# Two-layer hybrid encoder with eight experts: row counts in registers, another order of PE's expert code, and finer signals

## The chip, the cores and the metric

The kernel runs on one core of one Trainium2 chip. The metric is the device time of one execution in microseconds (us), as the median of several runs. TensorE is called PE here, VectorE DVE, ScalarE ACT, GpSimd POOL, and SP is the engine that issues most DMAs.

## What is computed

Two layers over 256 tokens of width 1024 in float32. Each layer has a token mixer (differential attention, an mLSTM and latent attention side by side) and a channel mixer. The second layer's channel mixer is the part that the change touches: each token goes to the best two of eight experts, and an expert is a SwiGLU of inner width 3584.

```python
def swiglu(u, wg, wu, wd):
    return (jax.nn.silu(u @ wg) * (u @ wu)) @ wd

    logits = (t @ w_router).astype(jnp.float32) + b_router.astype(jnp.float32)
    top_val, top_idx = lax.top_k(logits, TOP_K)
    gates = jax.nn.softmax(top_val, axis=-1)
...
        return swiglu(xblk, w_gate_e[e], w_up_e[e], w_down_e[e])
...
    y = jnp.zeros((n, d), h.dtype).at[tok_sorted].add(yb[dest] * g_sorted[:, None].astype(h.dtype))
```

Only the rows that chose an expert have to pass through it, but all of its weights do: 42 transfers of 1 MB an expert, 336 in all.

## The kernel before

The program is written engine by engine, and each engine runs its own instructions in the order in which they are written. Engines meet at semaphores alone: `then_inc` raises one when an instruction is done, `wait_ge` holds the engine until a value is reached.

**Routing.** Ahead of the experts, PE gathers the 512 chosen rows (two of each token) with selection matrices into eight PSUM banks (L1387). ACT copies the even banks into `xs`, DVE the odd ones (L1930 and L2542), and both raise `xs_ready`. The counts of rows of the experts stand in `cnt`, the first rows in `first`. POOL waits for eight `xs_ready`, and for each expert copies its rows, up to 256, from `xs` into `xe` (L2772) and raises `xe_ready`. In the profile `xs` shows as arena, `xe` as mixT.

**Which code an expert runs.** PE, ACT and DVE each hold six bodies of code, for up to 32, 64, 128, 160, 192 and 256 rows (`NVAR`), made by `experts` (L669). For each expert an engine jumps to "next", adds one to a register, jumps to "pick", loads the expert's count from `cnt` into a register (L684), and goes through a chain of tests ("tree") to the body that fits. The body of `first_variant`, 128 rows on all three engines, stands right behind the tests; the others follow in order of size. Each body begins with a hint for its own last jump, the one back to "next".

**A body.** It walks 14 stages of 256 inner columns. A stage's weights are three transfers into a ring of 14 slots of 1 MB: ("gu", s, 0) and ("gu", s, 1) hold gate and up for the upper and lower half of the 1024 inputs, ("down", s) the down product. Up to 64 rows PE works in plain float32 (`expert_whole`: gate and up at L1443, a turn at L1429, down at L1455). With more rows the weights are split into a high and a low part by ACT and DVE, and PE makes three products with 128-row or with wide tiles (`expert_split`, L1565 and L1613; `expert_wide`, L1484 to L1528). In both the first stage's gate and up is made whole (L1578, L1484).

**SP** issues the 42 transfers of an expert in a loop over the experts. Ahead of each it waits until the slot's last use is over (`last_use`, L789): a "down" block by `down_done`, both "gu" blocks of a stage by `gu_full`, which PE raises when the whole gate and up product of that stage is done.

## Time and profile before

| | us |
|---|---|
| median of 3 runs | 1678.16 (1676.92 to 1680.18) |
| profiled execution | 1674.14 |
| its span, first to last instruction | 1672.3 |
| PE busy with matmuls | 1478.1 (88%) |
| ACT busy | 589.6 (35%) |
| DVE busy | 781.4 (47%) |
| DMA of expert weights | 336 transfers of 1 MB |

Times of the trace are from the start of the span. The experts begin at about 680 us and end at about 1645. With these inputs the eight experts have, in order, up to 32, 32, 128, 64, 160, 32, 192 and 64 rows, which is seen in the shapes of PE's rows: 128x32 by 128x128 for 32 rows, 128x64 by 128x256 for 64, 128x512 for 128, and 128x160 and 128x192 for the wide ones. A row of the timeline merges equal instructions that follow each other. In brackets stands the idle time of the engine just before, and what ended it; "issue" is time in which the engine waited for nothing that the profile shows.

### The profile page before, as it was taken

The numbers are of one execution on the slowest core, as the hardware profiler recorded it, in microseconds if no ns is written. First come the engines' busy times: TensorE is split into PE (matmuls) and PEld (weight loads), VectorE is DVE, ScalarE is ACT, GpSimd is POOL, SyncE is SP. The second block draws the span as 40 slices with busy tenths as digits, with TensorE's granted clock in tenths as the row PEclk, the third lists the DMA queues.
The fourth block names the chain that finished last, engine by engine and source line by source line (L and its number), as shares of the span: only waits on it lengthen the run. The fifth ranks groups of instructions, "written<-read, shape, count | busy, mean of one in ns | idle before, by whom it ended". The sixth has DMA issues, their size and how long they took to land.

```text
span 1672.3 us, 30627 instructions
## 1 busy us (share of the span) xinstructions
PE 1478.1 (88%) x12402; PEld 1185.7 (71%) x12403; DVE 781.4 (47%) x1097; ACT 589.6 (35%) x793; POOL 69.4 (4%) x66
## 2 busy tenths in 40 slices
PE   5999899999999998756579999999996679999894
PEld 3878778999977886644458875588985468888452
DVE  2584565565546655100028851177761036665112
ACT  2445253444344432100027740156551025554101
POOL 0010100000010111000000000000000000000002
PEclk8999999999999999987789999999998789999998
DMA  9644467745433528899999999997567996555893
GB/s 362 236 161 175 192 229 291 287 170 196 158 100 123 227 76 362 350 424 424 424 424 426 426 410 426 424 406 285 236 281 306 424 424 245 225 226 227 328 426 151
DMA packets 69183, 488.89 MB, mean 292 GB/s; under 512 B 7744, under 2 KB 7776, under 8 KB 11168
## 3 DMA queue, kind: packets, MB, share of 16 engines
q1 hardware_dynamic: 66800, 479.94, 71.0%
q10 hardware_dynamic: 1648, 4.59, 0.8%
q8 instruction: 117, 1.92, 0.5%
q0 software_dynamic: 576, 2.10, 0.4%
q14 instruction: 42, 0.34, 0.1%
HBM read 482.66 MB, written 3.93 MB: 291 GB/s over the span
## 4 chain that ended last, share of the span: by engine, by line
PE 44%; DMA 9%; issue 4%; DVE 2%; SPq 1%; ACT 1%; POOL 1%; ACTq 0%; POOLq 0%; DVEq 0%
PE PG L1443 9%; DMA ring<-in_experts 6%; PE PG L1500 4%; PE Y L1528 4%; PE Y L1455 4%; PE TRB L1500 4%; PE PG L1565 4%; DMA arena<-in_experts 3%; PE TRB L1506 3%; PE PG L1506 3%; PE Y L1613 2%; PE Y L1519 2%; PE TRB L1429 2%; SPq L786 1%; PE Y L1252 1%
## 5 line engine op out<-in xcount | busy, mean ns | idle before, releaser
L2570 DVE COPY arena<-TRB 128x64 f32<-128x64 f32 (+1 forms) x70 | 17.6, 251 | 343.0 <-PE TRB L1429 343.0
L1443 PE MATMUL PG<-ring,mixT 128*32 128x128 f32 (+1 forms) x1920 | 117.4, 352 | 65.2 <-issue 60.6
L1677 ACT ACTIVATE rope<-PG 64x128 f32<-64x128 f32 (+2 forms) x84 | 27.2, 324 | 378.7 <-PE PG L1443 356.2
L1443 PEld LDWEIGHTS PG<-ring,mixT 128*32 128x32 f32 (+1 forms) x1920 | 90.6, 139 | 95.9 <-issue 81.4
L1677 ACT ACTIVATE parts<-ring 128x2048 fp32r<-128x2048 f32 x81 | 151.8, 1901 | 9.1 <-DMA ring<-in_weights 4.0
L945 PE MATMUL PG<-h_parts,parts 128*128 128x512 f32 x432 | 152.9, 394 | 1.4 <-DVE arena L2448 1.4
L1443 PE MATMUL PG<-arena,mixT 128*32 128x128 f32 (+1 forms) x1664 | 102.2, 353 | 42.0 <-issue 42.0
L1443 PEld LDWEIGHTS PG<-arena,mixT 128*32 128x32 f32 (+1 forms) x1664 | 79.2, 140 | 69.4 <-issue 56.3
L947 PE MATMUL PG<-h_parts,parts 128*128 128x256 f32 x432 | 121.9, 282 | 0.0
L2433 DVE TENSOR_TENSOR parts<-ring,parts 128x2048 fp32r<-128x2048 f32 x42 | 95.1, 2289 | 30.4 <-ACT parts L1677 30.4
L2554 DVE TENSOR_TENSOR parts<-arena,parts 128x2048 fp32r<-128x2048 f32 x42 | 95.2, 2287 | 17.0 <-PE Y L1519 14.4
L2554 DVE TENSOR_TENSOR ring_parts<-ring,parts 128x2048 fp32r<-128x2048 f32 x39 | 88.4, 2287 | 24.2 <-PE Y L1519 13.3
L945 PEld LDWEIGHTS PG<-h_parts,parts 128*128 128x128 f32 x432 | 81.2, 188 | 19.8 <-DVE arena L2448 1.6
L947 PEld LDWEIGHTS PG<-h_parts,parts 128*128 128x128 f32 x432 | 81.3, 188 | 0.0
L1677 ACT ACTIVATE parts<-arena 128x2048 fp32r<-128x2048 f32 x42 | 78.9, 1902 | 4.2 <-PE PG L1565 4.1
L912 PE MATMUL Y<-parts 128*128 128x256 f32 x224 | 63.5, 284 | 0.2 <-DVE parts L2457 0.2
L913 PE MATMUL Y<-parts 128*128 128x256 f32 x224 | 63.4, 283 | 0.0
L914 PE MATMUL Y<-parts 128*128 128x256 f32 x224 | 63.4, 283 | 0.0
L2123 DVE TENSOR_TENSOR ring_parts<-ring,ring_parts 128x2048 fp32r<-128x2048 f32 (+1 forms) x24 | 52.8, 2199 | 18.9 <-ACT ring_parts L1677 18.8
L2554 DVE TENSOR_TENSOR parts<-arena,scr_parts 128x2048 fp32r<-128x2048 f32 x21 | 48.1, 2292 | 26.6 <-ACT scr_parts L1677 26.6
L1455 PE MATMUL Y<-arena 128*32 128x256 f32 (+1 forms) x512 | 57.2, 450 | 1.8 <-DMA arena<-in_experts 1.8
L1677 ACT ACTIVATE ring_parts<-ring 128x2048 fp32r<-128x2048 f32 (+1 forms) x24 | 43.8, 1837 | 41.4 <-PE Y L1252 30.2
(384 smaller groups left out, 2839.8 us busy)
## 6 DMA issues: line engine op xcount, KB each, us to landing
ring<-in_experts SPq DMA_DIRECT2D x168, 1024.0 KB, 17.1
arena<-in_experts SPq DMA_DIRECT2D x168, 1024.0 KB, 18.9
ring<-in_weights SPq DMA_DIRECT2D x116, 1024.0 KB, 6.4
ring<-in_weights SPq DMA_DIRECT2D x4, 512.0 KB, 5.1
ypairs<-hT ACTq DMA_DIRECT2D x3, 512.0 KB, 7.0
tok<-in_x SPq DMA_DIRECT2D x1, 1024.0 KB, 9.0
result<-scr SPq DMA_DIRECT2D x2, 512.0 KB, 2.6
ring<-in_weights SPq DMA_DIRECT2D x2, 432.0 KB, 6.2
```

Source lines behind the costliest of these rows:

```text
L912: mm(out_, w_hi[w][:, c], x[0], start=first, stop=False, skip_group_check=True)
L945: mm(PG[:, m, :].rearrange("p (i t) -> p i t", i=2), w_hi[d % SPLITS][:, c], h_parts[:, :, k, :], start=(k == 0), stop=False, skip_group_c ...
L947: last = mm(PG[:, m, 0:T], w_lo[d % SPLITS][:, c], h_hi[:, k, :], start=False, stop=(k == KD - 1), skip_group_check=True)
L1443: last = mm(bank[i * n:(i + 1) * n, 0:width], xe[:, k, 0:n], w[k // 4][:, k % 4, i * width:(i + 1) * width], start=(k == 0), stop=(k == KD ...
L1455: last = mm(o, actT[:, s % 2, f, 0:n], w[:, f, c:c + width], start=(s == 0 and f == 0), stop=(s == STAGES - 1 and f == 1))
L1500: last = mm(both, hi[:, k, i // 2, i % 2, :], h_parts[:, :, h * KD // 2 + k, 0:n], start=(h == 0 and k == 0), stop=False, skip_group_check ...
L1506: last = mm(bank[:, 0:n], lo[:, k, i // 2, i % 2, :], h_parts[:, 0, h * KD // 2 + k, 0:n], start=False, stop=(h == 1 and k == KD // 2 - 1) ...
L1528: last = mm(o, a[:, s % 2, f, :], w[:, f, c:c + width], start=(opens and s == 0 and f == 0), stop=(closes and s == STAGES - 1 and f == 1))
L1565: last = mm(bank, x[j][:, h * KD // 2 + k, :], w[:, k, :], start=(opens and k == 0), stop=(closes and k == KD // 2 - 1))
L1677: return nc.scalar.activation(out_, in_, func, **kw)
L2433: V.tensor_tensor(w_lo[d % SPLITS], ring[:, slot_of[slot_of_dense(d)], :, :].rearrange("p k c -> p (k c)"), w_hi[d % SPLITS].bitcast(F32), ...
L2554: V.tensor_tensor(w_lo_e[q % SLOTS_E], ring_e[q % SLOTS_E].rearrange("p k c -> p (k c)"), w_hi_e[q % HI].bitcast(F32), ALU.subtract).then_ ...
```

## The change

1. **Counts in registers.** `experts` loads all eight counts into eight registers at the start. "next" adds one and moves each count one register down, and jumps straight to the tests. "pick" is gone. This holds for PE, ACT and DVE.
2. **32 rows behind PE's chain.** On PE, `first_variant` is 32: the tests ask for 256, 192, 160, 128 and 64 rows in turn, and the 32-row body follows them. ACT and DVE keep 128.
3. **A second hint.** On PE each body ends with a hint for the last test of the chain (`closest`), just ahead of the jump back. In the built program this test jumps to the 64-row body and falls through to the 32-row one.
4. **First rows in two pieces.** `xs_ready` becomes `xs_even` and `xs_odd`. Ahead of its loop POOL copies the first expert's rows as six of eight slices, then two, each when its banks are copied. The loop makes seven copies in place of eight.
5. **First blocks by own signal.** PE raises the new `gu_half` once the upper half of a stage's gate and up is done. SP waits for it ahead of refilling a ("gu", s, 0) slot, and DVE's `low_rows_of(0)` waits for it in place of `hi_used`. In the split and wide bodies the first stage's `hi_used` is raised one bank or one matmul earlier.

```diff
-            rows = eng.alloc_register(label("rows"))
+            to_come = [eng.alloc_register(label(f"rows_{i}")) for i in range(NE)]
+            rows = to_come[0]
+            for i in range(NE):
+                eng.reg_load(to_come[i], cnt[0:1, i:i + 1])
             eng.reg_mov(turn, 0)
-            eng.br(label("pick"))
+            eng.br(label("tree"))
             with nc.body(label("next"), valid_engines=own):
                 eng.reg_add(turn, turn, 1)
-                eng.br_lt(turn, NE, on_true=label("pick"), on_false=label("done"))
-            with nc.body(label("pick"), valid_engines=own):
-                e = eng.snap(turn, min_val=0, max_val=NE - 1)
-                eng.reg_load(rows, cnt[0:1, bass.ds(e, 1)])
-                eng.br(label("tree"))
+                for i in range(NE - 1):
+                    eng.reg_mov(to_come[i], to_come[i + 1])
+                eng.br_lt(turn, NE, on_true=label("tree"), on_false=label("done"))
...
-                        eng.br_lt(rows, NVAR[NVAR.index(n) - 1] + 1, on_true=then, on_false=label(n))
+                        closest = eng.br_lt(rows, NVAR[NVAR.index(n) - 1] + 1, on_true=then, on_false=label(n))
...
                     emit(eng.snap(turn, min_val=0, max_val=NE - 1), n)
+                    if name == "pe":
+                        closest.branch_hint(eng.mark_branch_hint_location())
                     eng.br(label("next")).branch_hint(back)
...
-                kind, s = expert_list[(i - SLOTS_E) % USES][0:2]
+                kind, s, *half = expert_list[(i - SLOTS_E) % USES]
+                if half == [0]:
+                    return gu_half, e * STAGES + ((STAGES if i >= SLOTS_E else 0) + s + 1)
...
+            pe.sem_inc(gu_half, STAGES)
...
+                        if k == KD // 2 - 1:
+                            last.then_inc(gu_half, 1)
...
-            experts(pe, "pe", expert)
+            experts(pe, "pe", expert, first_variant=32)
...
-                        ve.wait_ge(hi_used, e * USES + 1)
+                        ve.wait_ge(gu_half, e * STAGES + (STAGES + 1))
...
-            po.wait_ge(xs_ready, KD)
+            po.wait_ge(xg_full, KD)
+            rows = xs[:, 0:KD * PAIRS].rearrange("p (k s) -> p k s", k=KD)
+            for a, b in ((0, KD - 2), (KD - 2, KD)):
+                po.wait_ge(xs_even, b // 2)
+                po.wait_ge(xs_odd, b // 2)
+                last = G.tensor_copy(xe[:, a:b, :], rows[:, a:b, 0:T])
+            last.then_inc(xe_ready, 1)
             po.wait_ge(table_ready, 1)
-            with po.Fori(0, NE) as e:
-                start = po.value_load(first[0:1, bass.ds(e, 1)], min_val=0, max_val=PAIRS)
-                po.wait_ge(gu_full, e * FT + FT)
+            with po.Fori(0, NE - 1) as e:
+                start = po.value_load(first[0:1, bass.ds(e + 1, 1)], min_val=0, max_val=PAIRS)
+                po.wait_ge(gu_full, e * FT + 2 * FT)
```

How this stands on PE, from the last gather to the body behind the tests. Each row is the source line, the operation, its operands and how many follow each other. Before, with the 128-row body (L1578) behind the tests:

```order
1935 L1387 MATMUL TRB<-parts,h_parts 128x512 x8
1936 L678 UNCONDITIONAL_BRANCH
1937 L680 REGISTER_ALU
1938 L681 COMPARE_AND_BRANCH
1939 L683 ISA
1940 L684 TENSOR_LOAD cnt
1941 L685 UNCONDITIONAL_BRANCH
1942 L692 COMPARE_AND_BRANCH x2
1943 L694 COMPARE_AND_BRANCH x3
1944 L697 BRANCH_PREFETCH_HINT
1945 L698 ISA
1946 L1415 ISA
1947 L1578 MATMUL PG<-ring,mixT 128x512 x8
```

The same place now, with the 32-row body (L1451 now, L1443 before):

```order
1934 L1395 MATMUL TRB<-parts,h_parts 128x512 x8
1935 L680 TENSOR_LOAD cnt x8
1936 L682 UNCONDITIONAL_BRANCH
1937 L684 ISA
1938 L687 COMPARE_AND_BRANCH
1939 L696 COMPARE_AND_BRANCH x5
1940 L699 BRANCH_PREFETCH_HINT
1941 L700 ISA
1942 L1423 ISA
1943 L1451 MATMUL PG<-ring,mixT 32x128 x64
```

The load of a count has left the way from one expert to the next, and the 32-row body has taken the place of the 128-row body. The end of a body on PE shows the new hint; now the 32-row body's last product, its jump back, and the 64-row body that follows it:

```order
2015 L1465 MATMUL Y<-arena 32x256 x8
2016 L702 BRANCH_PREFETCH_HINT
2017 L703 UNCONDITIONAL_BRANCH
2018 L699 BRANCH_PREFETCH_HINT
2019 L700 ISA
2020 L1423 ISA
2021 L1451 MATMUL PG<-ring,mixT 64x256 x32
```

On POOL, ahead of the experts, the first copy is now in two pieces outside the loop (L2784), ahead of the load of `first`:

```order
35 L2777 MEMSET arena 128x512
36 L2784 COPY mixT<-arena 128x1536
37 L2784 COPY mixT<-arena 128x512
38 L2787 UNCONDITIONAL_BRANCH
39 L2787 ISA
40 L2788 TENSOR_LOAD first
```

Before, the loop began there, and its load and its copy of 128x2048 were the first.

The built program holds 64 bytes an instruction. The bodies of PE have 2,359 instructions for 32 rows, 1,293 for 64, 1,135 for 128, 2,677 for 160 and 2,454 for 192 before, each one or two more now.

## Rows read from the trace of the kernel before

**Rows 1.** From the page: its first line, and the queue that brings instructions
```profile
span 1672.3 us, 30627 instructions
...
q8 instruction: 117, 1.92, 0.5%
```

**Rows 2.** Timeline of PE, the first matmuls of each expert: start, us, what, [idle before]
```profile
679.85 5.25 PE L1443 MATMUL PG<-ring,mixT 128*32 128x128 f32 x128 [4.54 <-POOL mixT L2772]
...
766.11 6.84 PE L1443 MATMUL PG<-ring,mixT 128*32 128x128 f32 x128 [7.53 <-issue]
...
866.64 8.82 PE L1578 MATMUL PG<-ring,mixT 128*128 128x512 f32 x16 [2.44 <-issue]
...
991.03 7.13 PE L1443 MATMUL PG<-ring,mixT 128*64 128x256 f32 x64
...
1078.80 2.44 PE L1484 MATMUL PG<-mixT,ring 128*128 128x160 f32 x16
...
1265.14 6.13 PE L1443 MATMUL PG<-ring,mixT 128*32 128x128 f32 x128 [10.23 <-issue]
...
1352.08 4.53 PE L1484 MATMUL PG<-mixT,ring 128*128 128x192 f32 x16 [7.20 <-issue]
...
1559.60 9.14 PE L1443 MATMUL PG<-ring,mixT 128*64 128x256 f32 x64 [5.61 <-issue]
```

**Rows 3.** Stretches: length, busy PE, PEld, DVE, ACT, POOL, PE clock, DMA share, GB/s
```profile
680.00:690.00 10.00, 9.53 (x244) 8.50 (x244) 1.33 (x5) 2.09 (x4) 0.00 (x0) 0.85 0.52 201
690.00:700.00 10.00, 9.03 (x222) 6.55 (x214) 1.56 (x6) 0.81 (x3) 0.00 (x0) 1.00 1.01 424
...
980.00:990.00 10.00, 8.96 (x40) 7.13 (x39) 5.63 (x6) 2.69 (x3) 2.42 (x1) 1.00 1.01 413
990.00:1000.00 10.00, 10.00 (x85) 6.50 (x85) 1.84 (x4) 2.63 (x4) 0.00 (x0) 1.00 0.97 371
...
1265.00:1270.00 5.00, 4.86 (x92) 4.89 (x96) 0.00 (x0) 1.12 (x1) 0.00 (x0) 0.50 0.10 15
...
1345.00:1350.00 5.00, 0.00 (x0) 0.00 (x0) 1.80 (x3) 1.99 (x3) 0.00 (x0) 0.53 1.01 421
```

**Rows 4.** Chain of waits in the fourth expert: start, us, what
```profile
1040.66 3.45 PE PG L1443 x32
...
1046.62 3.47 PE PG L1443 x32
...
1052.60 1.25 issue
1053.86 3.67 PE PG L1443 x32
...
1060.04 1.14 issue
...
1067.35 1.11 issue
```

**Rows 5.** Timeline, all engines, the start of the fifth expert
```profile
1085.42 2.34 PE L1484 MATMUL TRB<-mixT,ring 128*128 128x160 f32 x16
...
1090.39 1.44 PE L1500 MATMUL PG<-h_parts,parts 128*128 128x320 f32 x8 [2.63 <-DVE rope L2601]
```

**Rows 6.** Timeline, the sixth expert: SP's first transfers and PE's last product
```profile
1268.97 7.65 SPq L786 DMA_DIRECT2D ring<-in_experts  x7
...
1343.81 1.07 PE L1455 MATMUL Y<-arena 128*32 128x256 f32 x16 [1.64 <-DMA arena<-in_experts]
```

**Rows 7.** Timeline, the sixth expert: weight loads (PEld) of one product
```profile
1277.75 1.31 PEld L1443 LDWEIGHTS PG<-arena,mixT 128*32 128x32 f32 x41
...
1280.54 0.59 PEld L1443 LDWEIGHTS PG<-arena,mixT 128*32 128x32 f32 x23 [1.49 <-issue]
```

**Rows 8.** Timeline ahead of the first expert: last gathers, copies, SP's first transfers
```profile
673.29 2.02 PE L1387 MATMUL TRB<-parts,h_parts 128*128 128x512 f32 x8
...
675.35 0.69 DVE L2542 COPY arena<-TRB 128x512 f32<-128x512 f32 x1 [1.17 <-PE TRB L1387]
677.71 1.89 POOL L2772 COPY mixT<-arena 128x2048 f32 x1 [23.60 <-issue]
...
683.56 7.42 SPq L786 DMA_DIRECT2D ring<-in_experts  x7
```

More of the change, by code:

```diff
@@ L589, in build @@
         xg_full = sem("xg_full")
-        xs_ready = sem("xs_ready")
+        xs_even, xs_odd = sem("xs_even"), sem("xs_odd")
+        gu_half = sem("gu_half")
         pad_zero = sem("pad_zero")
@@ L1486, in gate_up_whole @@
                             if i == 2:
-                                used = last
-                        (used if h else last).then_inc(hi_used, 1)
-                    last.then_inc(gu_full, 2)
+                                last.then_inc(hi_used, 1)
+                        last.then_inc(gu_full if h else gu_half, 2 if h else 1)
                 def gate_up_half(s, h):
@@ L1507, in gate_up_half @@
                                       start=False, stop=(h == 1 and k == KD // 2 - 1), skip_group_check=True)
-                    if h == 1:
-                        last.then_inc(gu_full, 2)
+                    last.then_inc(gu_full if h else gu_half, 2 if h else 1)
                 def down_rest(s):
@@ L1581, in gate_up_first @@
                                 last.then_inc(gu_full, step)
-                        (before if h else last).then_inc(hi_used, 1)
+                        before.then_inc(hi_used, 1)
+                        if h == 0:
+                            last.then_inc(gu_half, 1)
                 def gate_up(s):
@@ L1603, in gate_up_half @@
                     lo_ready(e, q)
-                    gate_up_part(s, h, x_hi, w_lo_e[q % SLOTS_E], closes=(h == 1))
+                    last = gate_up_part(s, h, x_hi, w_lo_e[q % SLOTS_E], closes=(h == 1))
+                    if h == 0:
+                        last.then_inc(gu_half, 1)
                 def down_part(s, a, w, opens=False, closes=False):
@@ L1927, in _ @@
                 ae.wait_ge(xg_full, k + 1)
-                run(xs[:, k * PAIRS:(k + 1) * PAIRS], xg_banks[k], ACT.Copy).then_inc(xs_ready, 1)
+                run(xs[:, k * PAIRS:(k + 1) * PAIRS], xg_banks[k], ACT.Copy).then_inc(xs_even, 1)
             for b in range(TB):
@@ L1931, in _ @@
             ae.wait_ge(table_ready, 1)
-            ae.wait_ge(xs_ready, KD)
+            ae.wait_ge(xs_even, KD // 2)
+            ae.wait_ge(xs_odd, KD // 2)
             def silu(e, n, u, m):
@@ L2541, in _ @@
                 ve.wait_ge(xg_full, k + 1)
-                V.tensor_copy(xs[:, k * PAIRS:(k + 1) * PAIRS], xg_banks[k]).then_inc(xs_ready, 1)
+                V.tensor_copy(xs[:, k * PAIRS:(k + 1) * PAIRS], xg_banks[k]).then_inc(xs_odd, 1)
             def gated(e, n, u, m):
@@ L2648, in expert_split @@
                 ve.sem_inc(conv_lo, 2)
-                ve.wait_ge(hi_used, e * USES + 1)
+                ve.wait_ge(gu_half, e * STAGES + (STAGES + 1))
                 low_rows_of(0)
```

## Prediction

> **What bounds the kernel now.** I read four views, in this order. The page first: one execution spans 1672.3 us [rows 1]. The rows of TensorE (PE) at the eight places where an expert begins [rows 2] then give the row counts of the experts by their shapes (32, 32, 128, 64, 160, 32, 192 and 64) and the idle time ahead of each: 4.54, 7.53, 2.44, none, none, 10.23, 7.20 and 5.61 us. Nothing in the profile is waited for in most of that ("issue"). The table of stretches says which of these gaps cost anything [rows 3]: weights come at 424 GB/s and the DMA engines are full (1.01) from 690 us on, still so at 980 and again at 1345; they idle in part at 680 to 690 (201 GB/s), a little at 990 to 1000 (0.97), and nearly wholly at 1265 to 1270 (0.10). So:
> - experts 1 and 2 are bound by DMA: their end is set by when the transfers restart near 683 us. The 7.53 us gap between them is hidden.
> - expert 3 (128 rows) is bound by PE from its first matmul. Expert 4 (64 rows) is too, until DMA is late three times: its stages begin 5.96 us apart (1040.66, 1046.62), then 7.24, with 1.25, 1.14 and 1.11 us of idle [rows 4]. PE alone would end it 3.5 us earlier.
> - expert 5 (160) is PE's own, and its start hangs on ScalarE and VectorE: PE has its four banks done about 1087.7 us but waits for VectorE until 1090.39 [rows 5], some 2 us of slack.
> - expert 6 (32 rows) is bound by DMA, which stood still before it: its first weights are asked for at 1268.97, and PE waits for the last at 1343.81 [rows 6]. Experts 7 and 8 are PE's. So the gaps of 10.23, 7.20 and 5.61 us all cost time, the 2.44 one too.
>
> **What a gap is made of.** The code of an expert has to be brought in: the instruction queue made 117 transfers of 1.92 MB, 16.4 KB each [rows 1]. The built program has 64 bytes an instruction, so a transfer brings a block of 256. PE stops after 41 of 64 loads in the middle of one product and goes on 1.49 us later with nothing to wait for [rows 7]. That is a block boundary reached before its block. Counted in the built program it is the 335th load of the 32-row code, and all boundaries follow from it. The 128-row code stands right behind the tests and its gap is 2.44 us; from the same 32-row code to a 32-row code that stands elsewhere it is 7.53. **A jump to code that is not there costs 7.53 - 2.44 = 5.1 us** (P). 10.23 us is more than that. The 160-row code jumps back 14 instructions behind a boundary, the other bodies 81 to 165, so there the hint given at the body's start can do little. **A late jump back costs 10.23 - 7.53 = 2.7 us** (B), and up to P while the DMA engines are full.
>
> [...]
>
> **The change part by part.**
> 1. First rows in two pieces. The copy of all rows took 1.89 us from 677.71, after the last VectorE copy ended at 676.04 [rows 8]. Now six of eight slices go once PE's last gather is done (673.29 + 2.02 = 675.3), about 1.45 us, then two in about 0.55 us (estimates from 1.89 us for eight, plus 0.1): ready near 677.4 against 679.6. The register load and the address work that stood ahead are gone too. PE starts 2.2 us sooner. Eight register loads at the start lie on PE behind queued gathers, and on ScalarE and VectorE before 681, when the first product is whole.
> 2. First blocks by own signal. SP may refill a slot after half a product instead of a whole one. Two products took 5.25 us [rows 8], so this is 1.3 to 1.6 us more; the first transfer goes from 683.56 [rows 8] to about 679.8. **Experts 1 and 2 end 3.8 us earlier** (ends: 2.2 and 4.6; 201 of 424 GB/s in ten us leaves 5.3 to gain). In steady DMA it gives nothing.
> 3. 32 rows behind the tests. The bodies of the built program now end 32 (32 rows), 47, 160, 24 and 176 instructions behind a boundary, against 137, 151, 81, 14 and 165. For 32 rows this boundary is 2 or 3 instructions behind the last wait for weights, so the jump back is late each time; before it was early.
>  - 32 to 32: hidden, as before.
>  - **32 to 128** was 2.44. It loses the place behind the tests (+5.1) and its early jump back (+2.7 to +5.1), less 0.4 for the register load (an estimate; no row shows one, and it is 0 to 2.44): +7.4 to +9.8, I take +8.2, nearer B since the block asked for meanwhile saves a little. Queued on PE behind it is expert 3, all of PE's, so nothing hides it.
>  - 128 to 64, 64 to 160: no jump fetches now. The 64-row code begins in the block where the 32-row code ends, and the 160-row code where the 128-row code ends. A late jump back after 64 rows, a little over 1 us beyond what is queued, falls into the 2 us of slack. ScalarE's way to expert 5 is 0.4 us shorter. Expert 4's late weights: half a product of 3.62 us and fuller slots take 2.4 of its 3.5 us.
>  - **160 to 32** was 10.23. The code follows the tests, but only 24 instructions of it lie in that block, and the next must come too; the second hint may put another transfer ahead of it. Between nothing and P is saved, plus 1.5 for the half signal (half of 3.1 us, from 6.84 us for two products [rows 2]): 1.5 to 6.6, I take 4.0.
>  - **32 to 192** was 7.20 and holds P already; add a late jump back: +2.3 to +4.7, with DMA full [rows 3] I take +3.6.
> 4. Second hint. The built program puts the last test's jump on 64 rows, so the hint names the 64-row code. **192 to 64** was 5.61: its block is asked for at the jump back, instead of another block first: -0.4 to -5.6, I take -2.4, since the transfer still has to come. A block of instructions has no row of its own, so this is a choice near the middle.
>
> Sum: -3.8 + 8.2 - 2.4 - 0.4 (to expert 5's end: +1.6) - 4.0 + 3.6 - 2.4 = **-1.2 us**. The profiled execution took 1674.14 us, 1.8 around its span, so 1672.9; it lies 4.0 under the median of 1678.16, and the difference, not the level, is forecast: 1677.0 us.
>
> **Rivals.**
> - A, slower. The jumps out of 32-row code are late at the full price. B is P when the DMA engines are full, and the block behind the tests costs as much as the jump did: +9.8, +4.7, -1.5 in place of +8.2, +3.6, -4.0: +5.2 more, 1682. For it: both jumps fall where the DMA share is 1.01 [rows 3]. Against: 7.53 was paid at the same share. It decides from B of about 4 us.
> - B, faster. The nearer hint brings the tests' block in time and the late jumps back vanish, or the boundaries lie a few instructions elsewhere: 2.7 less after each of two 32-row bodies, and 2 more after 160 rows: 1669.6. For it: four of the seven jumps back were in time. Against: the count.
> - C, slower. At 64 to 160 the 160-row code's block is no longer kept: it is ten transfers old, where it was the next block before. That is +5.1 and 1 us, less 1.7 of slack: 1681.4. For it: the 192-row code, twelve blocks back, paid 7.20. [...]
> - D. The change moves code and nothing of it shows at the end, since what the 32-row bodies gain the others lose: this is my sum itself.
>
> **How the numbers follow.** Forecast, with D in it, 0.45 (its own range 1674 to 1680), A 0.17, B 0.30, C 0.08. Leaving out a tenth at each side gives 1668.5 to 1684. A measurement tells 0.2%, 3.4 us, from no change. Faster: B and a little of the forecast, 0.32. Slower: A, C and a little, 0.24. Same: 0.44.
>
> **What would show it.** First PE matmul of expert 1 near 677.7 and SP's first transfer near 679.8. Idle ahead of the 128-row code of 10 us or more, of the 192-row code over 10, of the 64-row code at the end near 3, of the last 32-row code from 10.2 to about 7. Expert 3 begins about 4 us later than 866.64, expert 5 about 2 later than 1078.8. If the gap at 128 rows stays under 7 us, the count of boundaries is wrong and B holds; if a gap of 5 us opens at or shortly behind the 160-row code's start, C does; if the 32-row code stops after its first 20 matmuls for 5 us, A does.

## Result: 0.81% slower, and the profile after

Each kernel was timed several times beside the kernel before. The changed kernel takes 1695.15 us (median of 9 runs) against 1680.19 (9 runs); the ratio is 1.0081 with a 95% interval of 1.0062 to 1.0100, so 13.6 us **slower**. The forecast was 1.2 us faster, in a range that ended 5.8 us above the median of before; the result lies outside it.

The spans of the two profiled executions differ by more, 1672.3 against 1693.3 us, since the profiled execution of before was 6.0 us under its median and that of after on it. Part of the difference arises ahead of all that the change touches: PE's gathers began at 667.58 us before and at 669.75 after, and in the profiles of the experiments anywhere from 667.75 to 675.96. So starts are counted from the first gather on, and places are compared by their gaps.

The page of after: as many matmuls, and four blocks of instructions fewer.

```profile
span 1693.3 us, 30716 instructions
...
PE 1477.2 (87%) x12402; PEld 1183.5 (70%) x12402; DVE 781.6 (46%) x1096; ACT 589.9 (35%) x793; POOL 69.4 (4%) x67
...
q8 instruction: 113, 1.85, 0.4%
```

How much a transfer of that queue brings is seen in the trace of before, between the start of its second transfer and of its 37th, where PE has no record of a jump (columns as in [rows 3], then the queue):

```profile
43.52:657.98 614.46, 591.14 (x4417) 502.97 (x4416) 360.21 (x576) 253.79 (x401) 42.41 (x35) 0.99 0.51 194
...
q8 instruction: 35, 0.57, 0.4%
```

The matmuls and weight loads alone are 252 a transfer, and all records of PE with its waits and register instructions, 9,023, are 258. In the 160-row body, from 1087.47 to 1233.08 us, nine transfers began over 2,258 records, 251 each. So I take 256 instructions for a block of 16,384 bytes, 64 bytes each, and the stops lie where this puts them (e3). The bodies have their counted lengths in the trace too: from the hint at a body's start to the add behind its jump back there are 2,361 records of PE for 32 rows, 1,286 for 64, 1,118 for 128, 2,682 for 160 and 2,455 for 192, within 1.5% of the built program's counts (a trace can lack some records).

The timeline of PE in after, the first matmuls of each expert, which answers to [rows 2] (start, us, what, [idle before]):

```profile
679.92 1.03 PE L1451 MATMUL PG<-ring,mixT 128*32 128x128 f32 x10 [2.39 <-POOL mixT L2784]
683.65 4.87 PE L1451 MATMUL PG<-ring,mixT 128*32 128x128 f32 x118 [2.69 <-issue]
...
766.20 1.03 PE L1451 MATMUL PG<-ring,mixT 128*32 128x128 f32 x10 [6.47 <-issue]
772.36 4.89 PE L1451 MATMUL PG<-ring,mixT 128*32 128x128 f32 x118 [5.13 <-issue]
...
878.35 10.19 PE L1586 MATMUL PG<-ring,mixT 128*128 128x512 f32 x16 [12.38 <-issue]
...
1004.08 7.13 PE L1451 MATMUL PG<-ring,mixT 128*64 128x256 f32 x64
...
1099.32 4.22 PE L1494 MATMUL PG<-mixT,ring 128*128 128x160 f32 x16 [10.07 <-issue]
...
1280.05 0.63 PE L1451 MATMUL PG<-ring,mixT 128*32 128x128 f32 x10 [4.33 <-issue]
1286.83 5.35 PE L1451 MATMUL PG<-ring,mixT 128*32 128x128 f32 x118 [6.15 <-issue]
...
1374.70 5.19 PE L1494 MATMUL PG<-mixT,ring 128*128 128x192 f32 x16 [11.96 <-issue]
...
1580.66 8.81 PE L1451 MATMUL PG<-ring,mixT 128*64 128x256 f32 x64 [3.39 <-issue]
```

Three things are new in it. Ahead of the third expert stand 12.38 us in place of 2.44, ahead of the seventh 11.96 in place of 7.20. Ahead of the fifth, where there was no gap, stand 10.07. And each 32-row body stops after ten matmuls. Ten matmuls are 20 instructions (each has a weight load), with four others ahead of them behind the tests, which is where the block that holds the tests ends by the forecast's count. Place by place, in us of the two profiled executions:

| | before | after | difference | forecast |
|---|---|---|---|---|
| start of the gathers | 667.58 | 669.75 | +2.2 | 0 |
| gathers to the end of expert 2 | 196.6 | 196.2 | -0.4 | -3.8 |
| gap ahead of expert 3 | 2.44 | 12.38 | +9.9 | +8.2 |
| expert 3 | 124.4 | 125.7 | +1.3 | 0 |
| expert 4 | 87.8 | 85.2 | -2.6 | -2.4 |
| gap ahead of expert 5 | 0 | 10.07 | +10.1 | 0 |
| expert 5 | 176.1 | 176.4 | +0.3 | -0.4 |
| gap ahead of expert 6, and expert 6 | 90.0 | 87.0 | -3.0 | -4.0 |
| gap ahead of expert 7 | 7.20 | 11.96 | +4.8 | +3.6 |
| expert 7 | 201.9 | 202.6 | +0.7 | 0 |
| gap ahead of expert 8 | 5.61 | 3.39 | -2.2 | -2.4 |
| expert 8 and the end | 112.7 | 112.6 | -0.1 | 0 |

The differences add up to 21.0, while the medians are 15.0 apart: the table tells where time went, not how much of it to the microsecond. One line was not forecast at all, the 10.1 us ahead of the fifth expert.

### The profile page after: what moved, and what is told of

The parts are those of the page before. It is cut to its first block, busy times and chain, and to the rows that moved or that the text cites. A ratio compares the mean times of both kernels' runs of the same rounds, so it can differ in the third digit from the quotient of the medians.

```text
span 1693.3 us, 30716 instructions
## 1 busy us (share of the span) xinstructions
PE 1477.2 (87%) x12402; PEld 1183.5 (70%) x12402; DVE 781.6 (46%) x1096; ACT 589.9 (35%) x793; POOL 69.4 (4%) x67
## 4 chain that ended last, share of the span: by engine, by line
PE 45%; DMA 9%; issue 5%; DVE 2%; POOL 1%; ACT 1%; SPq 0%; POOLq 0%; ACTq 0%; DVEq 0%
PE PG L1451 9%; DMA arena<-in_experts 6%; PE PG L1509 4%; PE Y L1465 4%; PE Y L1536 4%; PE TRB L1509 4%; PE PG L1573 4%; DMA ring<-in_experts 3%; PE TRB L1515 3%; PE PG L1515 3%; PE Y L1625 2%; PE Y L1527 2%; PE TRB L1437 2%; PE PG L1494 1%; PE Y L1260 1%
## 5 line engine op out<-in xcount | busy, mean ns | idle before, releaser
L1451 PE MATMUL PG<-ring,mixT 128*32 128x128 f32 (+1 forms) x1920 | 115.5, 339 | 61.8 <-issue 59.4
L1451 PEld LDWEIGHTS PG<-ring,mixT 128*32 128x32 f32 (+1 forms) x1920 | 86.9, 133 | 94.0 <-issue 76.4
L1451 PE MATMUL PG<-arena,mixT 128*32 128x128 f32 (+1 forms) x1664 | 99.5, 344 | 43.8 <-issue 43.8
L1451 PEld LDWEIGHTS PG<-arena,mixT 128*32 128x32 f32 (+1 forms) x1664 | 76.8, 136 | 70.9 <-issue 57.8
L2136 DVE TENSOR_TENSOR ring_parts<-ring,ring_parts 128x2048 fp32r<-128x2048 f32 (+1 forms) x24 | 52.8, 2199 | 18.9 <-ACT ring_parts L1689 18.8
L1689 ACT ACTIVATE arena<-PG 128x512 f32<-128x512 f32 x29 | 17.4, 598 | 114.5 <-PE PG L955 105.6
```

Source lines behind the costliest of these rows:

```text
L1451: last = mm(bank[i * n:(i + 1) * n, 0:width], xe[:, k, 0:n], w[k // 4][:, k % 4, i * width:(i + 1) * width], start=(k == 0), stop=(k == KD ...
L1689: return nc.scalar.activation(out_, in_, func, **kw)
```

## Experiments

All twelve ran beside the kernel before; us are the ratio less one times 1680. The intervals are 2 to 4 us to each side, so two of these kernels are told apart by their times alone only where they differ by some 4 to 5 us.

| | ratio (95% interval) | us |
|---|---|---|
| changed kernel | 1.0081 (1.0062 to 1.0100) | +13.6 |
| e1_first128 | 0.9998 (0.9980 to 1.0016) | -0.3 |
| e2_onehint | 1.0080 (1.0057 to 1.0103) | +13.4 |
| e3_padded | 1.0003 (0.9986 to 1.0020) | +0.5 |
| e4_before_late | 1.0057 (1.0040 to 1.0074) | +9.6 |
| e5_signals | 0.9969 (0.9951 to 0.9987) | -5.2 |
| e6_registers | 0.9983 (0.9965 to 1.0000) | -2.9 |
| e7_no_order_no_hint | 0.9969 (0.9953 to 0.9985) | -5.2 |
| e8_tests_in_bodies | 0.9873 (0.9849 to 0.9896) | -21.3 |
| e9_160_behind_64 | 1.0040 (1.0023 to 1.0058) | +6.7 |
| e10_tests_unpadded | 0.9925 (0.9911 to 0.9939) | -12.6 |
| e11_all_engines | 0.9843 (0.9824 to 0.9862) | -26.4 |
| e12_e7_padded | 0.9946 (0.9925 to 0.9966) | -9.1 |

### Which part costs

**e1_first128**, the order alone undone.

```diff
-            experts(pe, "pe", expert, first_variant=32)
+            experts(pe, "pe", expert)
```

> The changed kernel with the 128-row body behind PE's tests again; all other parts of the change stay. Theory M (code blocks: a block of PE's code that is not there costs about 5 to 6 us while weights stream, and the new order of the bodies makes more of them be missed): the gap ahead of the third expert falls from 12.38 to about 2.5 us, that ahead of the fifth from 10.07 to none, that ahead of the seventh from 11.96 to about 7.2, and 10.2 us stand ahead of the sixth again. The time lies 3 to 7 us under the kernel before. Rival U (the cost comes from the other parts: registers, pieces, signals): the time stays 10 us or more over the kernel before.

Measured: 13.9 us less than the changed kernel, level with the kernel before. The order (part 2) carries the whole loss; theory M stands, U falls. The gaps came back as expected, none ahead of the fifth expert, 9.91 us ahead of the sixth and 7.67 ahead of the seventh. But the 3 to 7 us of gain did not come. The timeline of PE shows where one part of it went, in the 128-row body behind the tests (the stretch shown ends after 100 of the first row's 128 matmuls):

```profile
685.63 4.58 PE L1451 MATMUL PG<-ring,mixT 128*32 128x128 f32 x100 [5.39 <-issue]
...
871.46 4.55 PE L1586 MATMUL PG<-ring,mixT 128*128 128x512 f32 x10 [0.95 <-DMA ring<-in_experts]
881.44 5.28 PE L1586 MATMUL PG<-ring,mixT 128*128 128x512 f32 x6 [5.42 <-issue]
```

After ten matmuls a block ends, and PE stops for 5.42 us. The kernel before ran through the same place [rows 2]. The first line shows the other part: PE's first product waits for its jump, not for POOL.

**e7_no_order_no_hint**, the second hint taken out of e1.

```diff
-                    if name == "pe":
-                        closest.branch_hint(eng.mark_branch_hint_location())
```

> Parts 1, 4 and 5 (registers, pieces, signals), with the 128-row body behind PE's tests and one hint, as before. Theory H1 (a hint that is armed takes the place of the next block in order): the stop of 5.42 us in the 128-row code of e1_first128, after its tenth matmul, is gone, and so are 3 to 5 us of its time; the gap ahead of the last expert stays at 5.2 to 5.6. 3 to 5 us under the kernel before. Rival: the stop is of the moved block boundary alone; it stays, and the time is that of e1_first128.

Measured: 0.9969, 4.9 us less than e1 (just clear of the noise of the two), and the sixteen matmuls stand in one row:

```profile
867.37 7.13 PE L1584 MATMUL PG<-ring,mixT 128*128 128x512 f32 x16 [1.22 <-DMA ring<-in_experts]
```

The rival falls. The transfers of PE's code show the order: in e1 three blocks were brought here, beginning at 867.73, 873.45 and 879.05 us, in e7 two, at 863.68 and 869.24. The third of e1 began 3.0 us after PE had stopped (876.01). So I read it as follows: an armed hint takes the place of the next block in order. It is given at a body's end, the tests' block is entered, the hint's target is asked for, and the block right behind the tests is asked for only when PE stands at its border. That the block at 873.45 is the hint's target is inferred, since a transfer doesn't tell which block it brings.

**e2_onehint**, the same edit on the changed kernel.

> The changed kernel without the second hint. Theory H1 (the hint for the 64-row code takes the place of the next block in order): the 32-row code still stops after 10 matmuls, but for 2.5 to 3.5 us in place of 5.13 and 6.15, the gap ahead of the last expert rises from 3.39 to about 5.6, and the sum is 0 to 3 us less than the changed kernel. Rival H2 (the second hint is what makes the jumps back late): the jumps back after 32 rows cost about 1 us, the gap ahead of the third expert falls from 12.38 to about 8, and the time is over 10 us less than the changed kernel. Rival H3: the hint does nothing, all gaps stay within 0.5 us.

Measured: 1.0080, as the changed kernel. The single places came out near what H1 said (the rows from the second on):

```profile
678.40 3.70 PE L1449 MATMUL PG<-ring,mixT 128*32 128x128 f32 x128 [2.39 <-POOL mixT L2782]
...
765.96 5.23 PE L1449 MATMUL PG<-ring,mixT 128*32 128x128 f32 x118 [3.01 <-issue]
...
873.12 9.95 PE L1584 MATMUL PG<-ring,mixT 128*128 128x512 f32 x16 [12.92 <-issue]
...
1276.81 5.79 PE L1449 MATMUL PG<-ring,mixT 128*32 128x128 f32 x118 [2.28 <-issue]
...
1574.46 9.13 PE L1449 MATMUL PG<-ring,mixT 128*64 128x256 f32 x64 [6.19 <-issue]
```

The stops after ten matmuls fall from 5.13 to 3.01 and from 6.15 to 2.28, the last gap rises from 3.39 to 6.19. In this order the hint gives 2.8 us at one jump and takes 3.9 inside the sixth body. H2 falls with the 12.92: the jumps back are late without it too. The first row shows what H1 had not named: the first body's stop of 2.69 us is gone as well. SP's first transfer came 11.4 us behind the gathers in place of 15.6, and the second expert ended 191.9 us behind them in place of 196.2. At that place no body had given a second hint yet, so the reading above does not explain it; what ties this stop to the hint is open. The 4 us that this trace gains there are not seen in the ratio, and lie within the noise of the two (5 us).

**e5_signals**, parts 4 and 5 on the kernel before (`experts` as before, all else as changed).

> The kernel before with parts 4 and 5 alone (first rows in two pieces, first blocks by own signal). By the forecast: PE starts 2.2 us sooner, SP 3.8 us sooner, the third expert begins 3.8 us sooner, and 3 to 6 us are gained in all. Rival S1: the first 32-row product waits for the jump instead, which took 6.05 us and ends at 678.2 in the kernel before, 1.4 us ahead of the copy: then PE starts 1 to 1.5 us sooner and 1 to 3 us are gained. Rival S2: within 1 us of the kernel before, since the weights are late at the fourth expert whatever happens at the first.

Measured: 0.9969, 5.2 us faster (2.2 to 8.2), around the forecast's 3 to 6. Counted from the gathers at 672.24, SP's first transfer came 13.1 us behind them (16.0 before, 15.6 in the changed kernel) and PE's first matmul 11.0 (12.3 before). But the third expert began only 2.1 us sooner, not 3.8, so the total fits better than its parts. Rival S1 named the first place rightly, PE waits for its jump there:

```profile
683.20 5.12 PE L1448 MATMUL PG<-ring,mixT 128*32 128x128 f32 x128 [3.20 <-issue]
```

**e6_registers**, part 1 on the kernel before.

> The kernel before with part 1 alone (counts in registers). Theory L: the eight loads take 3.0 us behind the last gather's wait, one load took 0.5 us; the jump to the 32-row code, 6.05 us long and hidden before, begins 2.5 us later, and PE's first product 1 to 1.5 us later (from 679.6 on, counted with the gathers at 667.58). Each later gap is 0.4 to 0.5 us shorter (no load, one jump less), of which three count. Sum: within 1.5 us of the kernel before. Rival: the shorter way shows in full at each of seven places, 3 us faster.

Measured: 0.9983 (0.9965 to 1.0000), 2.9 us faster, on the rival's 3 us, though the interval takes in theory L's 1.5 too. In the trace of the changed kernel the eight loads take 0.50 us for the first and 0.30 for each other, from 673.35 to 676.37, behind the wait that lets the last gathers go. The kernel before was in its test's jump by 672.19. In e6 the first matmul came 13.1 us behind the gathers, 0.8 later than before. With the signals on top, e7 is no faster than e5, and its first matmul came 13.5 us behind the gathers in place of 11.0: it seems that the registers cost at the first jump what they save at later ones, which no run shows by itself.

### What a late jump back costs

**e4_before_late**, the kernel before with code that never runs, so that the boundaries lie elsewhere.

```diff
+            if name == "pe":
+                eng.br_lt(turn, 0, on_true=label("pad"), on_false=label("pick"))
+                with nc.body(label("pad"), valid_engines=own):
+                    for _ in range(8 * 186):
+                        eng.reg_add(turn, turn, turn)
+                    eng.br(label("next"))
```

> The kernel before with about 150 instructions that never run ahead of next, so that its 32-row body ends 31 instructions behind a boundary (137 before), the 64-row body 46 (151), the 128-row body 230 (81), the 160-row body 166 (14) and the 192-row body 62 (165). No instruction that runs differs. Theory M: the 2.44 us ahead of the third expert become 6.5 to 7.5, the 7.20 ahead of the seventh 12, and the 10.23 ahead of the sixth fall to 6.5 to 7. By the forecast's price of a late jump back (2.7 us) the first two would be 5.1 and 9.9. Sum by M: +4.5 +4.8 -3.6 = 5 to 6 us slower than before; by the forecast's price about 1.5 us slower; by rival N no difference.

Measured: 9.6 us slower than before (6.7 to 12.4), with the same instructions executed.

```profile
874.92 8.98 PE L1585 MATMUL PG<-ring,mixT 128*128 128x512 f32 x16 [6.22 <-issue]
...
1089.73 4.38 PE L1491 MATMUL PG<-mixT,ring 128*128 128x160 f32 x16 [5.02 <-issue]
...
1271.50 1.03 PE L1450 MATMUL PG<-ring,mixT 128*32 128x128 f32 x10 [5.21 <-issue]
1275.29 4.80 PE L1450 MATMUL PG<-ring,mixT 128*32 128x128 f32 x118 [2.76 <-issue]
...
1365.60 5.12 PE L1491 MATMUL PG<-mixT,ring 128*128 128x192 f32 x16 [11.90 <-issue]
```

Ahead of the third expert 2.44 became 6.22 (M: 6.5 to 7.5), ahead of the seventh 7.20 became 11.90 (M: 12), and 10.23 ahead of the sixth fell to 5.21 with a stop of 2.76 behind it (M: 6.5 to 7). M had left out the 64-row body, 46 instructions behind its boundary: 5.02 us where there was no gap. In the trace the records of the jumps back behind the 32-row bodies last 5.89, 5.75 and 5.30 us (0.89, 1.53 and 0.46 before), the one behind the 64-row body 5.81. The forecast's 2.7 is refuted for jumps at which weights stream.

**e3_padded**, the same kind of edit on the changed kernel (`8 * 74`, to "tree").

> The changed kernel with 65 instructions that never run between PE's first load of counts and the code of next, so that everything behind them lies 61 places further in its block: the bodies end 91 (32 rows), 107, 221, 86 and 239 instructions behind a boundary in place of 30, 46, 160, 25 and 178, and the tests stand 25 behind one. Theory M: the jumps back are in time: 12.38 ahead of the third expert falls to 7 to 8 us, 10.07 ahead of the fifth to 6 to 7, 4.33 with the later stop of 6.15 ahead of the sixth to 1 to 2 in all, 11.96 to about 7; the stops after 10 matmuls vanish, the first one (2.69) too. In all 20 to 25 us less than the changed kernel, 5 to 10 less than the kernel before. Rival N (it is not the place in the block but what the jump has to do, the longer way or the registers): the gaps stay within 1 us and so does the time.

Measured: 13.1 us less than the changed kernel, so the place in the block decides and N falls; but 1.0003, not 5 to 10 under the kernel before.

```profile
880.18 9.10 PE L1593 MATMUL PG<-ring,mixT 128*128 128x512 f32 x16 [10.22 <-issue]
...
1092.83 3.88 PE L1501 MATMUL PG<-mixT,ring 128*128 128x160 f32 x16 [4.27 <-issue]
...
1278.07 0.85 PE L1458 MATMUL PG<-ring,mixT 128*32 128x128 f32 x21 [3.30 <-issue]
1283.10 0.76 PE L1444 MATMUL TRB<-con,rope 64*128 64x128 f32 x2 [4.17 <-DVE rope L2568]
```

The stop after ten matmuls moved to one after 107, and did not vanish. Those 97 matmuls with their weight loads are 194 instructions, and with the 61 places of the edit 255: the stop stands at the next boundary. The jumps back after the first two 32-row bodies, 91 instructions behind a boundary, still lasted 5.28 and 4.09 us, the one after the third 1.33. A bad expectation of mine: 91 instructions of a 32-row body seem to be gone in less time than a block takes.

**e12_e7_padded**, the same edit on e7.

> e7_no_order_no_hint with 65 instructions that never run ahead of next, which moves every boundary 61 places: the bodies of PE end 146 (128 rows), 203 (32 rows), 218, 82 (160 rows) and 234 instructions behind one, against 85, 142, 157, 21 and 173. Theory M: the jump back after 160 rows (3.84 us) is in time, so the 10.22 us ahead of the sixth expert become 6.3 to 6.8; the other gaps change by less than 1 us, or the 8.90 ahead of the seventh falls by its late 1.3. Sum: 3.5 to 5 us less than e7, 8 to 10 under the kernel before. By the forecast's own price (2.7 us) 2.7 less. Rival (the seconds the changed places gain at one jump they lose as a stop inside the next body, as in e3_padded): within 1.5 us of e7.

Measured: 0.9946, 3.9 us less than e7, 9.1 under the kernel before. In e7 PE stood 9.82 us ahead of the sixth expert and 8.43 ahead of the seventh; here:

```profile
1268.89 3.18 PE L1456 MATMUL PG<-ring,mixT 128*32 128x128 f32 x52 [5.00 <-issue]
...
1353.86 4.52 PE L1499 MATMUL PG<-mixT,ring 128*128 128x192 f32 x16 [6.81 <-issue]
```

The jump back behind the 160 rows lasted 0.33 us in place of 3.84, as M said. The difference of the totals by itself lies within the noise of the two (4.4 us); with these two places, 4.8 (less a new stop of 0.54) and 1.6 us shorter, 65 instructions that never run are worth some 4 us.

### The gap ahead of the 160 rows

**e9_160_behind_64**, the bodies of the changed kernel in another order.

```diff
-            for n in sorted(NVAR, key=lambda n: n != first_variant):
+            for n in ([32, 64, 160, 128, 192, 256] if name == "pe" else sorted(NVAR, key=lambda n: n != first_variant)):
```

> The changed kernel with the 160-row body of PE ahead of the 128-row body, so that the 64-row code ends in the block in which the 160-row code begins. Bodies now end 30 (32 rows), 46, 167 (160 rows), 25 (128 rows) and 178 instructions behind a boundary. Theory M, place by place: ahead of the fifth expert the test's jump (6.13 us) is gone and the jump back (about 5.7) stays, 10.07 becomes 4 to 4.5; ahead of the fourth (none) the jump back comes late, 4.5 to 5.5; ahead of the sixth the jump back (3.73) is in time, 4.33 becomes 1, and the stop after 10 matmuls stays. Sum: 3 to 5 us less than the changed kernel, still 9 over the kernel before. Rival C0 (the chip keeps fewer blocks than the seven or eight between two uses, and the jump to 160 rows is late wherever the code stands): 10.07 stays.

Measured: 6.9 us less than the changed kernel. The timeline of PE has no gap at the fifth expert:

```profile
1088.80 3.65 PE L1465 MATMUL Y<-arena 128*64 128x512 f32 x16
1092.39 2.44 PE L1494 MATMUL PG<-mixT,ring 128*128 128x160 f32 x16
```

C0 falls: with its code in the block where the 64-row code ends, the jump costs nothing. Two details differ from what I expected. The jump back after 64 rows lasted 1.09 us, not 5.7, with the boundary in the same place; that is not explained, and it means that the gap of 10.07 vanished for two reasons, of which this run shows only one. And ahead of the fourth expert nothing opened, though the 128-row body ends 25 instructions behind a boundary: no block was brought between 978.01 and 1009.80 us, so the tests' block, brought at the second expert's end, was still there, and nothing could be late.

### No late block at all

**e8_tests_in_bodies.** Each body of PE ends with its own tests, and asks ahead for the one jump that it will take.

```diff
+                    def arm(n=n, places=places):
+                        at = label(f"arm_{n}")
+                        eng.br(f"{at}_32")
+                        tests_of(to_come[1], at, lambda m: label(f"hint_{n}_{m}"))
+                        for m in NVAR:
+                            with nc.body(label(f"hint_{n}_{m}"), valid_engines=own):
+                                places[m] = eng.mark_branch_hint_location()
+                                eng.br(label(f"run_{n}"))
+                        nc.switch_bb(label(f"run_{n}"))
...
+                    eng.br_lt(turn, NE, on_true=label(f"tail_{n}_32"), on_false=label(f"out_{n}"))
+                jumps = tests_of(to_come[0], label(f"tail_{n}"), label)
+                for m in NVAR[:-1]:
+                    jumps[m].branch_hint(places[m])
```

> A new version, from the changed kernel: each body of PE ends with tests of its own that jump straight to the next body; behind its first gate and up product it tests the next expert's count, which stands in a register, and gives the hint for that one jump; the counts are loaded between the two halves of the gathers; code that never runs puts every body's tests 150 instructions or more behind a block boundary and its start near one. Theory M: no block is asked for late: the gaps ahead of the second to eighth expert fall to 0.3 to 1.5 us each (before: 7.53, 2.44, 0, 0, 10.23, 7.20, 5.61), which gives 20 to 26 us less than the kernel before with the signals' gain. Rival (one hint among several that were given stays armed, or hints from a place so far ahead are lost): gaps of 5 to 7 us stay at each jump, and the time is within 5 us of the kernel before.

Measured: 0.9873, 21.3 us faster than before, as M said; 108 blocks brought in place of 117. The timeline of PE at the third and the eighth expert, and ACT ahead of the eighth's first product:

```profile
865.66 7.13 PE L1655 MATMUL PG<-ring,mixT 128*128 128x512 f32 x16
...
1538.98 7.13 PE L1518 MATMUL PG<-ring,mixT 128*64 128x256 f32 x64 [0.30 <-issue]
...
1549.42 1.28 ACT L1759 ACT_TABLE_LOAD   x1 [9.50 <-issue]
...
1551.68 1.22 PE L1504 MATMUL TRB<-con,rope 64*128 64x128 f32 x4 [5.58 <-DVE rope L2631]
```

PE's gaps are gone, and the next engine shows: ACT's code for the 64 rows comes late (6.10 us of its 9.50 lie between its last test, over at 1543.10, and the body's first record at 1549.20), and PE waits 5.58 us for what hangs on it (8.45 at the sixth expert). Before, ACT stood idle there too, for 10.13 us, but what ended it was PE's product, itself 5.61 us late.

**e10_tests_unpadded**, e8 without the padding (`PADS` of one each).

> e8_tests_in_bodies without the code that never runs. The tests at the end of the bodies now stand 61 (32 rows), 123, 27 (128 rows), 194 (160 rows) and 137 instructions behind a boundary, against 150 to 211. Theory M: the jump out of 128 rows is late by 4.5 to 5.5 us, each jump out of 32 rows by 4 to 5 us (two of the three count), the others are in time: 10 to 14 us more than e8, still 7 to 11 less than the kernel before. Rival (the tests and hints alone do it, wherever the blocks lie): within 2 us of e8.

Measured: 0.9925, 8.7 us more than e8. That is a little less than the 10 to 14 expected. The gaps are 4.32 us ahead of the third expert, 3.94 ahead of the seventh, 3.22 ahead of the eighth, and none at the fourth, where M had 4.5 to 5.5. So of e8's 21.3 us the pieces and signals bring 5.2 (e5), the tests, the hints and the registers 7.4, and the place of the blocks 8.7.

**e11_all_engines**, the same tests on ACT and DVE.

> e8_tests_in_bodies with the tests at the end of the bodies and the hint for the next jump on ACT and DVE too, there at the start of a body and without padding. In e8 PE stood 5.58 us at the eighth expert and 8.45 at the sixth for a DVE result that waited for ACT, whose code came 9.5 us late. If the hint works from the same block: both fall to 1 or 2 us, 4 to 8 us less than e8 (the stop at the sixth also waits for weights). If ACT's shorter bodies leave the hint no block to be given in, no more than 2 us less than e8.

Measured: 0.9843, 26.4 us faster than before, 5.1 less than e8, which is as much as the noise of the two. PE's waits bear it out: 8.45 us at the sixth expert became 3.18, and 5.58 at the eighth are gone. ACT and PE at the eighth expert:

```profile
1541.11 1.28 ACT L1765 ACT_TABLE_LOAD   x1 [4.04 <-issue]
...
1543.36 0.71 PE L1510 MATMUL TRB<-con,rope 64*128 64x128 f32 x4
```

This is the fastest version of the series.

## Why the prediction was wrong

**What held.** The view of the gaps, and that the code has to be brought in by blocks of 256 instructions (252 to 258 of them a transfer in the trace of before). PE's first product began 2.1 us sooner behind the gathers (10.2 for 12.3), for 2.2 forecast. The places of the boundaries: the forecast said "if the 32-row code stops after its first 20 matmuls for 5 us, A does", and it stopped after ten for 5.13 and 6.15. The prices of 32 to 192 (+4.8 for +3.6), 192 to 64 (-2.2 for -2.4) and of expert 4 (-2.6 for -2.4) are near. The forecast's 0.4 us for a load of a count was an estimate without a row; the eight loads in the trace of before last 0.30 to 0.59 us. The price of 160 to 32 (-3.0 for -4.0) is near by luck: PE's idle time there did not fall, 4.33 and 6.15 us stand in place of 10.23. SP's first transfer came 1.3 us sooner behind the fifth expert (12.8 for 14.1); where the rest came from is not shown.

**The step that failed first** is "128 to 64, 64 to 160: no jump fetches now. The 64-row code begins in the block where the 32-row code ends, and the 160-row code where the 128-row code ends." For 64 rows it held. For 160 it did not: the gap is 10.07 us, of which the trace's records give 5.74 to the jump back and 6.13 to the test's jump, less what was queued. This is rival C, to which I gave 0.08, and e9 shows it by its opposite: the code behind the 64 rows, no gap. Each of the two jumps is also seen late alone: with the test's jump late (5.84 us) and the jump back in time the gap was 4.27 (e3), with the jump back late (5.81) and the test's jump in time it was 5.02 (e4). Together that is 9.3 of the 10.07. The ground for 0.08 was the jump from 128 to 64 rows, which had shown no gap. In the trace of after, six blocks were brought between the one at 959.74, by its order the one with which the 128 rows end, and the jump to the 160 rows, and it was gone; six were brought as well behind the 32-row code's last block (857.62), and it was still there at the fourth expert. What decides between them stays open.

**The second** is "A late jump back costs 10.23 - 7.53 = 2.7 us". I took the difference of two gaps, one in which the DMA share fell to 0.82 and then to 0.30 (1255 to 1265 us) and one at 1.01, for the price of one cause. Behind 160 rows the jump back lasted 3.95 us in the trace of before; with the DMA engines full (1.01 or 1.02 while they last) the jumps back of e4 last 5.30 to 5.89 and those of after 5.70 to 5.76, behind 32 and 64 rows. The forecast carried part of it (+8.2 against +9.9), since it took more than B there, but it put the jump back after 64 rows, 5.74 us, into 2 us of slack.

**The third** is the start, "Experts 1 and 2 end 3.8 us earlier", of which 0.4 came. SP's first transfer stood 15.6 us behind the gathers, 16.0 before. The signal works (13.1 in e5). The new stop of 2.69 us after ten matmuls, in front of the half product for which SP waits, took it back: without that stop SP came at 11.4 and the second expert ended 4.7 us earlier than before (e2). I had named that border for 160 to 32 and not for the start. But the step from SP's start to the end of expert 2 is loose too: 2.9 us at SP gave 1.2 at that end in e5, and 3.9 gave none in e3. (The 5.25 us of two products, given to [rows 8], stand in [rows 2].)

**The chances.** A (late jumps at the full price) and C were set up as cases of which one happens. Both happened, on two grounds that don't exclude each other, A at its two jumps out of 32-row code (+9.9 and +4.8 for its +9.8 and +4.7) but not in full at 160 to 32 (-3.0 for its -1.5). Together +5.2 and +4.4 on the forecast are 1686.6, and with the start's 3.4 they are at 1690, where the measured ratio puts it (1691.8 on the median that the forecast stood on). That this sum fits so well is partly luck: in the traces the fifth expert alone has +10.1 where C had 4.4. A range that ends at the dearer of two rivals is too short when both can be true. The chance of faster, 0.32, rested on B, boundaries "a few instructions elsewhere"; they lay where they were counted.

**And the part of the change that did good** was real: parts 1, 4 and 5 are worth 5.2 us (e7). The order and the hint together cost 18.8 on top. In the new order the hint's share doesn't show (e2); in the old one it is 4.9 (e1 against e7).

## What to carry to other kernels

A jump to code that is not there cost 4 to 7 us here (4.21 in e7, 7.03 in e12). A body's place in its block decided whether its hint could hide the jump back: behind the first 32-row body it lasted 0.89 us at 137 instructions behind a boundary (before) and 5.89 at 31 (e4). So before code is put in another order, count where bodies end and where the tests stand. Here a last jump 137 instructions or more behind a boundary cost 1.6 us at most, one 81 to 86 behind was in time in the 128-row and 160-row bodies, and one 91 behind lasted 5.28, 4.09 and 1.33 us in 32-row code (e3). A hint was not free: with it the block behind the tests came 5.42 us late (e1). If the next target is known early, as a count in a register, test for it inside the body and hint that one jump: with that PE's gaps of 2.44 us ahead of the third expert and 5.61 ahead of the eighth were none and 0.30 (e8).

## What the hardware showed that I had not expected

- With the second hint the next block came late: 5.42 us inside the 128-row body with it (e1), none without (e7).
- A long gap costs once more through PE's clock. The stretches of after around the third expert's start (columns as in [rows 3]):

```profile
865.00:870.00 5.00, 0.96 (x16) 0.32 (x15) 1.54 (x3) 1.48 (x3) 0.00 (x0) 1.00 1.02 424
870.00:875.00 5.00, 0.00 (x0) 0.00 (x0) 0.00 (x0) 2.66 (x3) 0.00 (x0) 0.59 1.01 424
875.00:880.00 5.00, 1.65 (x2) 0.84 (x3) 0.00 (x0) 0.00 (x0) 0.00 (x0) 0.50 1.01 421
880.00:885.00 5.00, 5.00 (x8) 1.97 (x7) 0.00 (x0) 1.13 (x1) 0.00 (x0) 0.55 1.01 423
885.00:890.00 5.00, 5.00 (x16) 2.78 (x15) 4.29 (x5) 2.14 (x3) 0.00 (x0) 1.00 1.02 429
```

After 12.38 us of idle the granted clock is 0.50, and the first sixteen matmuls take 10.19 us in place of 8.82. Those 8.82 hold some of it too: behind 1.22 us of idle, with 1.00 granted throughout, they take 7.13 (e7). At the fifth expert, with 0.50 granted from 1095 to 1100 us, they take 4.22 in place of 2.44.
- Instructions that never run change the time by up to 0.8%: -13.1 us (e3 against the changed kernel), +9.6 (e4 against the kernel before), and -3.9 (e12 against e7), the last within the noise of the totals and borne out by its gaps.
- With PE's code in time, ACT stood idle for 9.50 and 9.65 us at the eighth and the sixth expert (e8), 6.10 and 6.50 of it between its last test and its body's first record; with hints on that engine too it was 4.04 and 4.11 (e11).
